# Loading and summing the routed rows during the last experts, and computing the values before turning the queries, in one hybrid attention and expert layer

## What is computed

```python
h = rmsnorm(x, norm1_g) * (1 + scale1) + shift1
q_lat, ckv, k_rope, conv_in, gate_logits = split(h @ w_in)
q = rmsnorm(q_lat) @ w_uq            # 16 heads of 64 + 32 channels; the 32 are rotated
k_nope, v = decompress_kv(rmsnorm(ckv), w_ukv)
attn = softmax attention @ w_o_attn; conv = conformer branch (31 taps, layernorm) @ w_pw2
x = x + gate1 * ((g_attn * attn + g_conv * conv) @ w_out)
h2 = rmsnorm(x, norm2_g) * (1 + scale2) + shift2
# mixture of experts: 64 experts, 8 of them for each token, FF 256
routed = sum over the token's 8 experts of gate * (silu(h2 @ wg[e]) * (h2 @ wu[e])) @ wd[e]
x = x + gate2 * (routed + shared_expert(h2))
y = rmsnorm(x, final_g)
```

## Time and profile before

| what | value |
|---|---|
| median of 3 runs | 1272.62 us (1272.45 to 1274.0) |
| profiled execution, its own time | 1271.95 us |
| span in its profile, first to last instruction | 1270.1 us |
| TensorE busy (matmul) | 1121.3 us, 88% |
| VectorE busy | 1069.1 us, 84% |
| ScalarE busy | 802.5 us, 63% |
| GpSimd busy | 222.8 us, 18% |
| mean of DMA over the span | 260 GB/s |
| mean granted TensorE clock | 0.946 of full speed |

### The profile page before, as it was taken

One profiled execution on the slowest core, in us unless ns is written; L12 is line 12 of the kernel. 1 busy time (PEld: TensorE's weight loads), 2 busy tenths in 40 slices (PEclk: granted clock), 3 DMA queues, 4 the chain that ended last, 5 costly groups with the idle time before them and its releaser, 6 DMA issues.

```text
span 1270.1 us, 16915 instructions
## 1 busy us (share of the span) xinstructions
PE 1121.3 (88%) x5670; PEld 937.8 (74%) x5670; DVE 1069.1 (84%) x1454; ACT 802.5 (63%) x1005; POOL 222.8 (18%) x154
## 2 busy tenths in 40 slices
PE   4999999779989985788999999999999999999700
PEld 1799999645558974777888888888888888888600
DVE  5769999999976727557999999999999999999458
ACT  6543334667775413336888888888888888888401
POOL 1000000300000010011423232332332333232100
PEclk9999999899999998598999999999999999999955
DMA  9663556334446155337999999999999999999296
GB/s 349 188 162 100 151 158 164 101 99 145 156 130 202 67 213 205 120 133 291 370 362 378 378 362 377 374 368 354 363 349 353 365 380 357 363 379 353 85 356 239
DMA packets 124876, 330.22 MB, mean 260 GB/s; under 512 B 26200, under 2 KB 67831, under 8 KB 99863
## 3 DMA queue, kind: packets, MB, share of 16 engines
q1 hardware_dynamic: 101856, 294.06, 63.5%
q0 software_dynamic: 20144, 31.75, 6.9%
q10 hardware_dynamic: 2824, 3.74, 0.9%
HBM read 328.22 MB, written 43.24 MB: 292 GB/s over the span
## 4 chain that ended last, share of the span: by engine, by line
PE 61%; DVE 19%; DMA 13%; ACT 3%; issue 3%; SPq 1%; ACTq 0%; POOLq 0%; DVEq 0%
PE bank L1575 18%; PE bank L1577 17%; PE bank L1576 17%; DMA raw<-in_exp_w_down_dram 8%; PE bank L1585 5%; DVE lgu L1460 3%; DVE lo L1065 3%; DVE zb L1163 2%; DVE lo L1466 2%; DMA raw<-in_w_out_dram 1%; DVE slots L1529 1%; ACT hi L977 1%; DMA slots<-sh_d 1%; DVE mx L1238 1%; DMA raw<-in_mod_w_dram 1%
## 5 line engine op out<-in xcount | busy, mean ns | idle before, releaser
L1460 DVE TENSOR_TENSOR lgu<-raw,hgu 128x2048 fp32r<-128x2048 f32 x128 | 291.9, 2281 | 6.0 <-ACT hgu L970 6.0
L970 ACT ACTIVATE hgu<-raw 128x2048 fp32r<-128x2048 f32 x128 | 245.1, 1915 | 5.0 <-DMA sh_d<-shy 5.0
L1575 PE MATMUL bank<-hgu,xgh 128*128 128x512 f32 x512 | 206.5, 403 | 2.9 <-DVE lgu L1460 2.8
L1577 PE MATMUL bank<-hgu,xgl 128*128 128x512 f32 x512 | 201.2, 393 | 0.0
L1576 PE MATMUL bank<-lgu,xgh 128*128 128x512 f32 x512 | 199.9, 390 | 0.0
L1466 DVE TENSOR_TENSOR lo<-raw,hi 128x2048 fp32r<-128x2048 f32 x64 | 147.4, 2304 | 34.4 <-ACT hi L977 34.1
L1065 DVE TENSOR_TENSOR lo<-raw,hi 128x2048 fp32r<-128x2048 f32 (+3 forms) x61 | 133.1, 2185 | 50.0 <-ACT hi L742 49.9
L709 POOL DMA_INDIRECT y_d<-ys,ixt x64 | 129.5, 2023 | 55.1 <-ACT ys L1008 35.3
L977 ACT ACTIVATE hi<-raw 128x2048 fp32r<-128x2048 f32 x64 | 122.9, 1920 | 24.7 <-DMA raw<-in_exp_w_down_dram 24.6
L742 ACT ACTIVATE hi<-raw 128x2048 fp32r<-128x2048 f32 (+3 forms) x61 | 111.2, 1828 | 40.3 <-DMA raw<-in_w_out_dram 21.9
L1163 DVE SCALAR_TENSOR_TENSOR zb<-zb,cwt 128x400 f32<-128x400 f32 x240 | 135.3, 627 | 0.6
(11 more groups left out here) (288 smaller groups left out, 2141.0 us busy)
## 6 DMA issues: line engine op xcount, KB each, us to landing
raw<-in_exp_w_gate_dram SPq DMA_DIRECT2D x64, 1024.0 KB, 11.6
raw<-in_exp_w_up_dram SPq DMA_DIRECT2D x64, 1024.0 KB, 7.9
raw<-in_exp_w_down_dram SPq DMA_DIRECT2D x64, 1024.0 KB, 10.6
raw<-in_mod_w_dram SPq DMA_DIRECT2D x20, 1024.0 KB, 5.2
slots<-y_d SPq DMA_DIRECT2D x6, 2048.0 KB, 15.5
raw<-in_w_in_dram SPq DMA_DIRECT2D x16, 512.0 KB, 5.4
raw<-in_w_in_dram SPq DMA_DIRECT2D x8, 1024.0 KB, 5.3
mraw<-in_mod_w_dram SPq DMA_DIRECT2D x4, 1024.0 KB, 15.8
```

Of the source, the lines that this page charges most:

```text
L970: act.activation(hgu[k % 2][:, :, w, :], src, ACT.Copy).then_inc(ghi_done, 1)
L1460: dve.tensor_tensor(lgu[k % 2][:, :, w, :], src, hgu[k % 2][:, :, w, :].bitcast(F32), ALU.subtract).then_inc(glo_done, 1)
L1575: pe.matmul(out, ah, bh, start=first, stop=False)
L1577: return pe.matmul(out, al, bh, start=False, stop=last)
```

## The change

- **Tail.** The sum is no longer made from six blocks but slot by slot. Slot 0 of all tokens is loaded straight into `acc`; slots 1 to 7 and the shared expert's rows are loaded each into a tile of its own and added to `acc` by `plus(n, t)`, one instruction of 128x1024 for each slot and token tile. A slot n is final when expert 56 + n of the last eight has been scattered (`final`), so loads are issued during the last experts, into tiles whose weights are used up: slots 0 and 1 in SyncE's step 6 ahead of the last down weights (`first_rows`), slots 2, 3, 4, the shared rows and `tg` after it, each behind waits; slots 5, 6, 7 and the residual token tile by token tile, slots 5 and 6 into the tiles of 1 and 2. Slots 5, 6, 7 are added in `finished(t)`. `final_g` is loaded on ScalarE's queue before the expert loop, and a square root on ScalarE stands ahead of the tail.
- **Last two experts.** Their down weights are split to `hi[0]`, `lo[0]` and `hi[1]`, `lo[1]`, the place of expert 62's gate and up weights, and this is done in ScalarE's step 7, as soon as expert 62's gate and up product is done (`down_place`). Expert 62's down product goes to banks 2 and 3 (`down_banks`), so it doesn't wait for banks 6 and 7.
- **Front.** The eight `uv` groups stand before `qT`; `V` lies on the place of `x`, and VectorE does 13 taps before the `qT` copies and 12 after. GpSimd's copy of the key part becomes a DMA that reads one head 15 times. `modr2` lies on all partitions elsewhere, and its rows are added to `mod_d` by 32 DMAs of 2 KB: the first 16 as the blocks come, the other 16 after all of these. Since the new place overlaps `lnr` and `zf`, ScalarE waits for all 32 (`mod_rows_out`, 544) before the square root of the layer norm.

```diff
+    g += [("uv", kt, b) for kt in range(4) for b in range(2)]
     g += [("qT", h) for h in range(H)]
-    g += [("uv", kt, b) for kt in range(4) for b in range(2)]
...
+        def down_place(k, last):
+            return k % 2 if last else 3 * (k % 2) + 2
+        def down_banks(k, last):
+            return (psum[2], psum[3]) if last and k == UNROLL - 2 else (psum[6], psum[7])
...
+                if left == 2:
+                    first_rows(i)
                 if left > 1:
                     load_down(i, k + 1)
...
+            def first_rows(last):
...
+                sp.wait_ge(glo_done, before_last)
+                sp.wait_ge(scattered[0], even)
+                sp.wait_ge(scattered[1], odd)
+                sp.dma_start(acc[:, :, :], rows[:, :, 0, :]).then_inc(row_in[0], 16)
+                for a, b, tile in tb[1]:
+                    if a:
+                        sp.wait_ge(glo_done, last_gate)
+                    sp.dma_start(tile[:, :, :], rows[:, a:b, 1, :]).then_inc(row_in[1], 16)
...
+            def final(k):
+                sp.wait_ge(scattered[k % 2], sent[k // 2 + 1])
+                sp.wait_ge(scattered[1 - k % 2], sent[(k + 1) // 2])
+            sp.wait_ge(xt_filled, N)
+            final(2)
+            for a, b, tile in tb[2]:
+                if a:
+                    sp.wait_ge(glo_done, last_up)
+                sp.dma_start(tile[:, :, :], rows[:, a:b, 2, :]).then_inc(row_in[2], 16)
+            sp.wait_ge(dn_filled, N3)
+            final(3)
+            for a, b, tile in tb[3]:
+                sp.dma_start(tile[:, :, :], rows[:, a:b, 3, :]).then_inc(row_in[3], 16)
+            sp.wait_ge(gu_filled, N)
+            final(4)
+            sp.dma_start(tb[4][0][2][:, :, :], rows[:, :, 4, :]).then_inc(row_in[4], 16)
             sp.wait_ge(sh_out, 16)
+            sp.dma_start(tb["sh"][0][2][:, :, :], sh_d).then_inc(row_in["sh"], 16)
+            sp.wait_ge(dn_filled, N2)
...
+            for t in range(NT):
+                for k in (5, 6, 7):
+                    if k == 7:
+                        sp.dma_start(tx[:, t, :], x1_d[:, t, :]).then_inc(row7_in[t], 16)
+                    if t == 0:
+                        final(k)
+                    sp.wait_ge(sum_done, 3 * (k - 4))
+                    sp.dma_start(row_tile(k, t), rows[:, t, k, :]).then_inc((row7_in if k == 7 else rows56_in)[t], 16)
...
-            pool.tensor_copy(kT[ND:HD, 1:H, :], kT[ND:HD, 0:1, :].to_broadcast([RD, H - 1, 512])).then_inc(krep_done, 1)
+            pool.dma_start(kT[ND:HD, 1:H, :], kT[ND:HD, 0:1, :].to_broadcast([RD, H - 1, 512])).then_inc(krep_done, 16)
...
-            pool.wait_ge(mod_done, 12)
             for part in range(2):
-                for cc in range(2):
-                    pool.dma_start(mod_d[cc:cc + 1, :], modr2[2 * cc + part:2 * cc + part + 1, :], accum_op=ALU.add,
-                                   max_dma_last_dim=4096).then_inc(mod_rows_out, 16)
-                pool.wait_ge(mod_rows_out, 64 + 32 * part)
+                for i in range(8):
+                    rows, cols = mod_block(i)
+                    pool.wait_ge(mod_done, 5 + i)
+                    for cc in range(2):
+                        q = rows.start + 2 * cc + part
+                        pool.dma_start(mod_d[cc:cc + 1, 512 * i:512 * i + 512], modr2[q:q + 1, cols],
+                                       accum_op=ALU.add).then_inc(mod_rows_out, 16)
+                pool.wait_ge(mod_rows_out, 32 + 256 * (part + 1))
...
+                if left == 1:
+                    down_hi(i, k - 1, last=True)
                 if from_step(j, 3):
-                    rows_out(i, k - 3)
+                    rows_out(i, k - 3, last=left <= -1)
+                if left == 1:
+                    down_hi(i, k, last=True)
...
+                if left == 1:
+                    dve.wait_ge(row_in[0], 16)
+                    for t in range(NT):
+                        plus(1, t)
+                if left == 0:
+                    plus(2, 0)
...
+            plus(2, 1)
+            plus(2, 2)
+            for n in (3, 4, "sh"):
+                for t in range(NT):
+                    plus(n, t)
+            finished(0)
+            finished(1)
+            normed(0)
+            finished(2)
+            normed(1)
+            normed(2)
```

More of the change, by code:

```diff
@@ L879, in _ @@
                     act.activation(V[:, kt, 512 * b:512 * b + 512], p[:, :], ACT.Copy).then_inc(v_done, 1)
+            for h in range(0, H, 2):
+                p = got(act, ("qT", h))
+                act.activation(qT[:, h, :], p[0:HD, 0:T], ACT.Copy).then_inc(qT_act, 1)
             def exps(h):
@@ L1483, in hidden, with plus @@
                                          op0=ALU.mult, op1=ALU.mult).then_inc(hd_done, 1)
+            sums = {"all": 0}
+            def plus(n, t):
+                if n in row_in:
+                    dve.wait_ge(row_in[n], 16 * len(tb[n]))
+                else:
+                    dve.wait_ge((row7_in if n == 7 else rows56_in)[t], 32)
+                if t in sums:
+                    dve.wait_ge(sum_done, sums[t])
+                sums["all"] += 1
+                sums[t] = sums["all"]
+                dve.tensor_tensor(acc[:, t, :], acc[:, t, :], row_tile(n, t), ALU.add).then_inc(sum_done, 1)
             def hidden_lo(i, k):
@@ L1739, in _ @@
                     end(("uv", kt, b), ins)
+            pe.wait_ge(qtok_done, 9)
+            pe.wait_ge(qrope_done, 1)
+            for h in range(H):
+                p = begin(("qT", h))
+                for t in range(NT):
+                    ins = turn(p[0:HD, P * t:P * t + P], qtok[:, t, HD * h:HD * h + HD])
+                end(("qT", h), ins)
             pe.wait_ge(kT_done, H)
-            pe.wait_ge(krep_done, 1)
+            pe.wait_ge(krep_done, 16)
             pe.wait_ge(qT_act, H // 2)
@@ L1943, in turn_hidden, with down @@
                 ins.then_inc(ht_filled, 1)
-            def down(i, k):
-                j, s = i * UNROLL + k, 3 * (k % 2) + 2
+            def down(i, k, last=False):
+                j, s = i * UNROLL + k, down_place(k, last)
+                banks = down_banks(k, last)
                 pe.wait_ge(hdl_done, j + 1)
                 pe.wait_ge(dlo_done, j + 1)
-                if from_step(j, 1):
+                if last and k == UNROLL - 1:
+                    pe.wait_ge(ys_done, j - 1)
+                elif from_step(j, 1) and not last:
                     pe.wait_ge(ys_done, j)
@@ L1965, in step @@
                     gate_up(i, k)
-                if from_step(j, 1) and left >= 0:
+                if from_step(j, 1) and left >= 1:
                     turn_hidden(i, k - 1)
-                if from_step(j, 2) and left >= -1:
+                if from_step(j, 2) and left >= 1:
                     down(i, k - 2)
+                if left == 0:
+                    turn_hidden(i, k - 1)
+                    down(i, k - 2, last=True)
+                if left == -1:
+                    down(i, k - 2, last=True)
             turn_tokens(0, 0)
```

177 lines of the change are left out of this document (75 added, 102 removed).

## The result

| what | before | after |
|---|---|---|
| median | 1272.53 us (4 runs, 1270.62 to 1274.0) | 1239.56 us (4 runs, 1238.37 to 1240.93) |
| ratio to before, 95% interval | | 0.9742 [0.9725, 0.9759] |
| profiled execution, its span | 1271.95, 1270.1 us | 1239.66, 1237.9 us |
| TensorE, VectorE, ScalarE, GpSimd busy | 88, 84, 63, 18% | 91, 86, 65, 19% |
| mean of DMA | 260 GB/s | 268 GB/s |

The change saves 33.0 us; 37.4 were forecast. A time forecast in the clock of before is compared after taking 4.12 from it.

A forecast was written before the change was run, and what follows sets the result against it. DMA at nine tenths through the experts, then 60.5 us behind the last scatter, and a front stall. Span 1270.1 - 33.0 (tail) - 4.9 (front) + 0.5 (expert entry) = 1232.7; profiled 1234.6, median 1235.2; 8 in 10 from 1229 to 1245.

The forecast's parts named there:

- The tail's mechanism: After the last experts: routed rows largely travel in the expert loop's DMA gap, VectorE becomes the bound; gain 33.0 us.
- I take 1201 for it: Tail, last scatter: assumed time for the copy of expert 63, queued until scatter 61, landing anywhere from 1197.4 to 1205.3, frees `ys[1]`.
- landing on the path: Rival for the tail: scatters land late under full-rate row loads; price up to 12.7 us, 1247.9, middle 1243; chance 17%.
- The loads: Tail: slots 0 and 1 in by about 1184.5, slot 4 at 1199, shared rows 1203, `tg` 1206, the remainder 1223.
- slots 0 to 4 landed before 1200: Sign that the forecast is right: these tail loads are in before 1200 in the clock of the earlier trace.
- The last down product: End of the expert loop: expert 63's down product ends at 1198.7, against 1201.57 before; 2.9 us won.
- up to 3: Last experts: cost in us if the loads are 3 us late, less 1.9 us of slack; otherwise they cost nothing.
- The sums: Tail on VectorE: adds of 1.15 us, or 1.27 linked; 2.1 us lost before tile 0's row 7; ends at 1234.1.
- Front, stall: Ahead of attention: without GpSimd's copy, VectorE's 6.60 us instruction takes 0.32 and the rotation ends 6.3 us earlier; DMA costs 0.
- Front, order: Ahead of attention: with values before queries, 48 transposes take 5.5 us and attention on VectorE starts 4.9 us earlier.
- Modulation rows: Front: last 16 GpSimd DMAs start at 370.4, 0.77 us each, done 384.7, needed 399.76; margin 15 us, cost 0.
- The rival that could have made the kernel slower: Late modulation rows: ScalarE waits for all 32; 1257.6 at 3.11 us an issue, 1285 at 4.83; chance 3% middle, 1% slower.

The follow-up runs named there:

- hold: Changed kernel with the loads of slot 4, the shared rows, `tg` and everything behind them waiting until scatter 62 has landed: 1244.8 us, ratio 0.9771.
- ys3: Changed kernel with a tile and a semaphore of its own for expert 63's rows, so their copy doesn't wait for scatter 61: 1237.3 us, ratio 0.971.
- pool_copy: Changed kernel, new order kept, with GpSimd's copy of the key part again in place of the DMA: 1244.47 us, ratio 0.977.
- order_back: Changed kernel, key copy still a DMA, with queries ahead of values again and 3 and 22 taps: 1239.31 us, ratio 0.973.
- tail_only: Changed kernel with the stretch ahead of the experts as it was before the change: 1245.23 us, ratio 0.9771.
- front_only: Kernel before with only the stretch ahead of the experts changed, tail and last experts as before: 1265.03 us, ratio 0.9932.
- after_again: The changed kernel itself, unedited, run again beside later variants: 1239.96 us, ratio 0.9735 to the kernel before.
- best: Changed kernel with slots 5 and 6 of all tiles first, an own tile for expert 63's rows, and queries ahead of values: 1239.06 us, ratio 0.9733.
- down_first: Changed kernel with slot 1's loads issued behind expert 63's down weights, and slot 1's sums in the next step: 1241.21 us, ratio 0.9748.
- tg_late: Changed kernel with the two loads of `tg` moved behind the loads of slots 5 and 6 of tile 0: 1240.64 us, ratio 0.9736.

## Why the prediction was right or wrong

- *The tail's mechanism was right.* Slots 0 to 4 travel in the gap of the earlier trace rows, VectorE adds beside the last experts, and the tail length falls by 28.2 us. Forecast were 33.0 (and 4.9 of the front, less 0.5).
- *The scatters' landing was mis-sized.* The forecast, in the clock of after: scatter 61 issued 1190.71, landed 1196.88, 63's issued 1198.78, landed 1204.78, row 7 of tile 0 there at 1208.18. Measured: 1190.67, 1200.49, 1202.49, 1209.30 and 1212.94. So 61's landing took 9.82 us where I took 6.2 (3.6 of the miss), copy and issue 2.00 for 1.9, 63's landing 6.81 for 6 (0.8), and the load 3.63 for 3.4. Along this chain, the one that ended last, the sum is 4.8 us, and the end is 4.8 late: 1234.79 for 1229.98. From row 7 on the forecast was exact: 21.8 us of VectorE, measured 1234.79 - 1212.97 = 21.8. The step that failed is "I take 1201 for it", a value in the middle of 3.1 and 10.5; the median of 10.5 in the earlier trace rows came from scatters under the load that the change brings to this place, and it was the nearer row. `hold` shows that the load does it. The rival *landing on the path* had the right cause and a price of up to 12.7; it came to 4.8.
- *The loads were late too,* which the account of that one chain hides. In the clock of before, the larger part of slot 1 was issued at 1177.0 as forecast, but was in at 1187.7 instead of 1184.5; then came expert 63's down weights at 1190.3 for 1187.5, slot 2 at 1195.0 for 1191, slot 3 at 1198.8 for 1195, slot 4 at 1203.2 for 1199, the shared rows at 1207.5 for 1203, and `tg` at 1210.4 for 1206. The 6 us for 63's landing rested on the shared rows' ending about 1203, and the sign "slots 0 to 4 landed before 1200" did not come true. VectorE had added the shared rows at 1206.87 in the clock of after, where 1203.6 follows from the forecast. With two adds more it would have stood at about 1209.4, against the 1208.18 forecast for row 7: with every scatter on time some 1.2 of the 4.8 us would still have been lost. That is an estimate; no run shows it. (The slices at nine tenths in the earlier trace rows are 20 to 37 and not 21 to 36; nothing in the sum rests on it.)
- *An earlier scatter of 63 would not have saved it.* I had not seen that row 6 of tile 0 comes as late as row 7, nor that the loads of slots 0 to `tg` keep the queues at a share near 1: issued from 1170.1 to 1191.3, they land 9.0 to 15.0 us after their issue. `ys3` took the named chain away and won 0.1 us of tail, so the 3.6 us of scatter 61 are not what its landing cost; behind it stood the scatter of 62 and slot 6, which the prediction priced nowhere.
- *The last down product* was to end 2.9 us earlier. It ended at 1195.60 + 0.39 = 1195.99, 39.9 us after scatter 57; before, the copy that waited for it began at 1201.57, 41.3 us after the earlier trace rows: 1.5 earlier. Expert 63's down weights were split at 1186.22 instead of 1183.4, behind the backlog, and VectorE's hidden rows came at 1188.43 instead of 1186.21, 2.2 late, within the "up to 3" that the prediction gave. It cost nothing, since the copy of 63 waited 6.81 us anyway. So the freed tiles for the down weights gave no time here by themselves; this is argued from that wait and not shown, for a version without them wasn't tried, since slot 3's rows lie where the old tiles were.
- *The sums.* The adds of 1024 columns follow each other at 1.14 us unlinked and 1.26 linked (1214.23 - 1212.97), forecast 1.15 and 1.27. From the last expert on VectorE lost 4.83 us in waits for rows, where one of 2.1 was forecast.
- *Front, stall:* right, 6.60 to 0.33 us, and `pool_copy` shows the cause. The copy costs attention's start 3.4 us in the new order (`pool_copy` against after) and 6.8 in the old (before against `order_back`). The DMA in the copy's place, issued at 228.09, landed 7.7 us later, long before the first scores.
- *Front, order:* the size was right (48 transposes in 5.40 for 5.5, attention 5.36 us earlier from the turn of the keys for 4.9), but the credit was not. I worked out both edits together and never the DMA alone; `order_back` shows that the DMA alone gives 6.8 us to attention's start and that the new order takes back 1.4.
- *Modulation rows:* right. 16 issues took 12.54 us, 0.78 each for 0.77, and end at 377.1. ScalarE's square root began at 395.89; its queue had waited 2.89 us for VectorE and not for these rows. The rival that could have made the kernel slower is out. (That rival says that the trace has both sizes of an issue; it has the longer one, 3.11, but its shorter one is 0.96 and not 0.62.)
- *Expert entry:* ScalarE's issue took 0.34 us, and the entry comes 6.14 us earlier from the turn of the keys, 0.8 more than attention's start; I didn't trace these. The 0.5 us charged for the issue can't be told: `tail_only`, with the issue, enters 0.6 us later than the kernel before, and after, with it, 0.4 earlier than `front_only`. Nor can the 1.1 us lost in the expert part be told from its spread: from the entry to scatter 57 it is 581.48 us before and 582.58 in after, but 583.56 in `after_again`, 581.11 in `best`, 581.90 in `tail_only` and 581.94 in `front_only`.

## What to carry to other kernels

Work that is moved under a loop brings its bytes with it: price every transfer that stays on the path by the rows measured under load, here 8.6 to 10.3 us for the scatter of 61 and not the 3 to 4 us of a scatter when the queues are nearly idle. Before one transfer is made earlier, list what arrives just after it: two chains that end together need both edits. Where a tail moves its bytes at full rate, don't expect much of another order; here none of the orders tried gained anything that the runs can tell. And don't take the chain that ended last for the whole cost of its links. And when a stall and an order are changed together, cost each alone: the order here was a remedy for a stall that the other edit had removed.

## What the runs showed of the hardware

- A scatter of 128 rows of 4 KB landed after 3.1 us with the DMA share at 0.23 (`hold`), and after 8.6 to 11.0 where loads kept it at 0.9 or more for most of the time (`hold`, after, `ys3`, `down_first`). The scatter of 61 took 8.6 to 10.3 us in all eleven profiles with the loads beside it (8.6 in `down_first`, 10.34 in `tg_late`), and 4.1 in `hold`. A load of 0.5 MB issued within 2.6 us after 4.5 MB on the same queue took 15.68 us.
- A GpSimd copy of 32x7680 held one VectorE instruction for 6.60, 6.60 and 6.61 us in three kernels, after others with two inputs in SBUF had passed in its first 4 us (2.28 us for one of 128x2048, as elsewhere); a DMA that does the same holds GpSimd for 0.72.
- The spans of the same loop differ by up to 2.5 us between executions of different kernels (581.11 to 583.56) and by 1.0 between two of one kernel (582.58, 583.56), which is more than most of the edits tried here would bring.
